# Attention values with the values stationary and the probabilities moving, in three attentions of a two-block transformer kernel

## The chip, the cores and the metric

The kernel runs on one core of a Trainium2 chip. The metric is the device time of one launch in microseconds. The whole of two transformer blocks (512 tokens, width 1024) is one program.

## The reference

The first block has an attention with three branches (compressed, selected and window), a short convolution, an attention over a memory and a gated feed-forward. The second has a banded attention, an mLSTM and a feed-forward of 16384 experts. The change touches three attentions, the window and the selected branch of the first block and the band of the second. Each has 8 heads of 64 and 512 queries; in the first block 4 heads share one group of keys and values. For one branch the reference computes

```python
lg = jnp.einsum('bqghd,bkgd->bqghk', q_c, kw_c).astype(jnp.float32) * scale + bias_w
p_win = masked_softmax(lg, mask_w[:, None, None, :], -1)
o_win = jnp.einsum('bqghk,bkgd->bqghd', p_win, vw_c.astype(jnp.float32))
out = g_c[..., 0:1] * o_cmp + g_c[..., 1:2] * o_sel + g_c[..., 2:3] * o_win
```

What is changed is how the second product, probabilities by values, is placed on TensorE. All of it is in float32.

## The kernel before

The code writes a stream of instructions for each engine by hand, with semaphores between them. Nothing plans the order: on each engine it is the order in the code.

An attention is 32 *units*, one for a tile of 128 queries and one head, in the order of query tiles; eight units of one tile are a *group*, and a group's values fill one PSUM bank, 4 or 5 in turn. A unit of query tile t has n blocks of 128 keys: n = 1, 2, 3, 4 for the four tiles in the selected and the band attention (`causal_blocks`), 1, 2, 3, 3 in the window (`win_blocks`). Units go in pairs. The two units of a pair take their queries and keys from the two halves of the partitions.

- TensorE (`attend` of the tensor block, 2247 to 2294). In turn `pair` it issues the scores of units 2 pair and 2 pair + 1 (`score`, line 2245: 64 rows of the array each, up to 512 moving columns), then, for each half, the values of a unit two pairs back (line 2270: the turned probabilities are stationary, 128 columns, and 64 columns of values move; n matmuls) and the transposes of a unit one pair back (line 2260). A float32 matmul is two records in the trace, a transpose is one. `keep_busy` (line 2124) fills known gaps.
- VectorE (`attend` of the vector block, from 1545) adds the bias to the scores, takes the row minimum and writes the logits to SBUF (line 1560). When a group's eight values are there (`pv_done`) it calls `leave` (1523 to 1543), which multiplies the bank by the reciprocal sums and gates into `o_tok` or `oa_tok` and signals `head_out`.
- ScalarE (`softmax`, from 986) in each turn: the exponential of unit 2 pair (line 982), the copy of the turned probabilities of unit 2 pair - 2 from PSUM to `probT` (line 999), then the same for 2 pair + 1 and 2 pair - 1. Between turns `after` issues other things in the selected attention: high halves of the convolution and squares of `o_tok` rows.
- `probT` has two places, one for each parity of the unit; banks 2 and 3 hold the transposes.

Behind the window TensorE computes the compressed branch's logits (2399 to 2404), VectorE shifts them (1640 to 1643), ScalarE takes their exponential, VectorE sums them (1647) and adds the compressed values to `o_tok` (1541, 1543), and the selected attention's logits follow on VectorE. Behind the selected attention TensorE sums the memory's squares (line 2449), multiplies the convolution's half of the output projection (line 2145), then turns `o_tok` (2437), which VectorE has normalised (1678). Behind the band attention TensorE has one projection (line 2145) before it turns `oa_tok` (2655). A fourth attention (memory, `U_MEM`) uses the same functions and is not changed.

What the sequence of one turn is, in the code:

```python
for half in range(2):
    if pair >= 2:
        values(2 * (pair - 2) + half)
    if (2 if after_turn else 1) <= pair <= units // 2:
        turn_prob(2 * (pair - 1) + half)
```

## Time and profile before

| | us |
|---|---|
| median of 3 runs | 2499.01 |
| lowest, highest | 2495.87, 2500.77 |
| the profiled execution's own time | 2498.93 |
| its span | 2497.1 |
| TensorE (matmul) busy | 2449.4 |
| VectorE, ScalarE, GpSimd busy | 1579.0, 961.2, 1298.8 |

The span runs from the first to the last recorded instruction; 1.8 us of the time lie around it. The page and the timelines give starts in microseconds from the start of the span. PE is TensorE's matmuls, PEld its weight loads, DVE VectorE, ACT ScalarE. In a timeline, neighbouring records of one line are one row: the first number is the first record's start, the second the time to the last one's end, and xN their count. A record's end is modelled, with the pipeline's length in it, so the next row can begin before it; the distance of two starts is the time that a group takes. L2145 is the kernel's main product, used by all projections.

### The profile page before, as it was taken

What the parts mean: (1) busy time and instruction counts of PE and PEld (TensorE: products, weight loads), DVE (VectorE), ACT (ScalarE), POOL (GpSimd) and SP (SyncE); (2) the same over time, 40 slices, a digit from 0 to 9 for tenths busy, and PEclk for the clock granted to TensorE, in tenths of its full rate; (3) what the DMA queues carried; (4) which work ended last, traced back from release to release, by engine and by line L of the source; (5) the groups of instructions that cost most, each with busy time, mean ns of one, the idle gap of its engine ahead of it and who ended that gap; (6) DMA issues with size and microseconds to landing.
All of it is one profiled execution on the core that took longest, in us unless ns stands there. A gap on an engine that the chain in (4) does not pass through costs nothing.

```text
span 2497.1 us, 32817 instructions
## 1 busy us (share of the span) xinstructions
PE 2449.4 (98%) x12349; PEld 2071.3 (83%) x12349; DVE 1579.0 (63%) x2572; ACT 961.2 (38%) x1565; POOL 1298.8 (52%) x686
## 2 busy tenths in 40 slices
PE   9999999999999999999999999999999999999998
PEld 6877766778786777788789999999999888888886
DVE  2246354766402735332479887998940699999995
ACT  3256455222223435523333333434333433333333
POOL 3650323444454433144435787766666576766662
PEclk9999999999999999999999999999999999999999
DMA  5320112665433222122223898999998899999992
GB/s 215 118 76 10 58 62 87 197 197 177 152 103 124 77 84 68 35 93 93 101 85 117 295 299 285 357 353 360 356 324 259 299 363 364 360 369 363 365 364 87
DMA packets 212733, 508.91 MB, mean 204 GB/s; under 512 B 18400, under 2 KB 101344, under 8 KB 212192
## 3 DMA queue, kind: packets, MB, share of 16 engines
q1 hardware_dynamic: 123696, 338.22, 38.9%
q0 software_dynamic: 36864, 134.23, 15.1%
q10 hardware_dynamic: 52016, 34.36, 4.4%
q8 instruction: 99, 1.62, 0.3%
q14 instruction: 58, 0.48, 0.1%
HBM read 454.31 MB, written 52.43 MB: 203 GB/s over the span
## 4 chain that ended last, share of the span: by engine, by line
PE 89%; POOL 3%; DVE 3%; ACT 3%; DMA 1%; issue 1%; ACTq 0%; DVEq 0%; SPq 0%
PE bank L2145 72%; PE bank L2709 3%; PE bank_and L2145 3%; POOL weight_split L823 3%; PE bank L2270 3%; PE bank_and L2113 2%; PE bank L2260 1%; ACT weight_split L964 1%; DMA ring<-weights 1%; PE bank_and L2245 1%; PE bank L2245 1%; PE bank L2124 1%; POOL weight_split L839 0%; PE bank_and L2522 0%; PE bank L2581 0%
## 5 line engine op out<-in xcount | busy, mean ns | idle before, releaser
L2145 PE MATMUL bank<-h_split,weight_split 128*128 128x384 f32 (+1 forms) x5568 | 1134.6, 362 | 16.7 <-POOL weight_split L823 7.6
L2145 PEld LDWEIGHTS bank<-h_split,weight_split 128*128 128x128 f32 x5568 | 994.6, 188 | 130.7 <-POOL weight_split L823 14.7
L823 POOL TENSOR_TENSOR weight_split<-ring,weight_split 128x1024 fp32r<-128x1024 f32 x182 | 454.0, 2495 | 727.2 <-ACT weight_split L964 727.0
L2145 PE MATMUL bank<-late_weight_split,weighted_split 128*128 128x512 f32 x2268 | 514.9, 389 | 0.8 <-DVE weighted_split L2047 0.8
L2145 PEld LDWEIGHTS bank<-late_weight_split,weighted_split 128*128 128x128 f32 x2268 | 425.6, 188 | 89.3 <-issue 1.2
L850 POOL DMA_INDIRECT arena<-weights,arena x256 | 313.4, 1224 | 146.3 <-DVE arena L1899 59.5
L839 POOL TENSOR_TENSOR weight_split<-ring,weight_split 128x1024 fp32r<-128x1024 f32 x129 | 310.4, 2407 | 121.6 <-ACT weight_split L1336 120.8
L964 ACT ACTIVATE weight_split<-ring 128x1024 fp32r<-128x1024 f32 x182 | 191.9, 1054 | 291.0 <-PE bank L2145 273.0
L1336 ACT ACTIVATE weight_split<-ring 128x1024 fp32r<-128x1024 f32 x130 | 137.6, 1059 | 388.2 <-PE bank L2145 377.9
L2041 DVE TENSOR_TENSOR arena<-arena 128x384 f32<-128x384 f32 x128 | 226.9, 1773 | 20.2 <-DMA arena<-expert_acts 19.9
L839 POOL TENSOR_TENSOR late_weight_split<-ring,late_weight_split 128x1024 fp32r<-128x1024 f32 x63 | 151.9, 2411 | 103.5 <-ACT late_weight_split L1336 102.7
L1899 DVE CUSTOM_DVE_ANT_0 arena<-arena,bank_and 128x1024 f32<-128x1024 f32 x128 | 153.0, 1217 | 53.3 <-DMA arena<-weights,arena 52.1
L1370 ACT ACTIVATE weighted_split<-arena 128x384 fp32r<-128x384 f32 x128 | 67.3, 526 | 269.9 <-DVE arena L2041 269.9
L2031 DVE SCALAR_TENSOR_TENSOR bank_and<-arena,bank_and 128x1024 f32<-128x1024 f32 x127 | 162.7, 1281 | 0.9
L1336 ACT ACTIVATE late_weight_split<-ring 128x1024 fp32r<-128x1024 f32 x126 | 132.6, 1052 | 46.5 <-PE bank L2145 45.0
L2145 PE MATMUL bank<-hidden_layer_split,weight_split 128*128 128x512 f32 x528 | 122.3, 392 | 1.3 <-POOL weight_split L823 1.0
L2145 PEld LDWEIGHTS bank<-hidden_layer_split,weight_split 128*128 128x128 f32 x528 | 98.3, 188 | 25.0 <-issue 2.6
L1501 DVE SCALAR_TENSOR_TENSOR arena<-bank,rstd 128x512 f32<-128x512 f32 x42 | 29.0, 691 | 126.0 <-PE bank L2145 117.8
L2047 DVE TENSOR_TENSOR weighted_split<-arena,weighted_split 128x384 fp32r<-128x384 f32 x128 | 74.1, 580 | 47.5 <-ACT weighted_split L1370 47.5
L2709 PE MATMUL bank<-arena 128*128 128x128 f32 x768 | 93.4, 275 | 0.0
L2709 PEld LDWEIGHTS bank<-arena 128*128 128x128 f32 x768 | 92.3, 192 | 0.0
L2270 PEld LDWEIGHTS bank<-arena 128*128 128x128 f32 x528 | 67.4, 191 | 24.9 <-ACT arena L999 16.5
(354 smaller groups left out, 2713.0 us busy)
## 6 DMA issues: line engine op xcount, KB each, us to landing
ring<-weights SPq DMA_DIRECT2D x493, 512.0 KB, 4.5
expert_acts<-arena SPq DMA_DIRECT2D x128, 192.0 KB, 4.2
gates_spread<-arena ACTq DMA_DIRECT2D x24, 1024.0 KB, 12.9
arena<-gates_spread SPq DMA_DIRECT2D x96, 256.0 KB, 6.7
arena<-expert_acts SPq DMA_DIRECT2D x128, 192.0 KB, 6.7
arena<-weights,arena POOLq DMA_INDIRECT x256, 7.2
arena<-bias_sel ACTq DMA_DIRECT2D x1, 2048.0 KB, 7.6
arena<-bias_band ACTq DMA_DIRECT2D x1, 2048.0 KB, 7.9
```

The lines of the kernel that those rows point to most:

```text
L823: nc.gpsimd.tensor_tensor(w_split[:, (count - 1) % 2, 1, :], ring[:, n % RING, :], w_split[:, (count - 1) % 2, 0, :], ALU.subtract).then_i ...
L839: nc.gpsimd.tensor_tensor(w[:, 1, :], ring[:, (BEFORE + e) % RING, :], w[:, 0, :], ALU.subtract).then_inc(w_lo_ready, 1)
L850: nc.gpsimd.indirect_dma_start(gathered_rows[:, j % GR, :], None, expert_rows, bass.IndirectOffsetOnAxis(ap=pick, axis=0)).then_inc(gather ...
L964: a.activation(w_split[:, s % 2, 0, :], ring[:, n % RING, :], ACT.Copy).then_inc(w_high, 1)
L1336: a.activation(split_of(e)[:, 0, :], ring[:, n % RING, :], ACT.Copy).then_inc(w_hi_ready, 1)
L1899: v.tensor_tensor_reduce(rows_, rows_, wide[:, :], 1.0, 0.0, ALU.mult, ALU.add, dots[:, j:j + 1]).then_inc(gather_used, 1)
L2031: v.scalar_tensor_tensor(out=wide[:, :], in0=rows_, scalar=coef[:, j:j + 1], in1=wide[:, :], op0=ALU.mult, op1=ALU.add).then_inc(gather_us ...
L2041: v.tensor_tensor(weighed[:, e % 2, :], act_in[:, e % AS, :], gblk[:, b % 2, :, j], ALU.mult).then_inc(weighed_ready, 1)
L2047: v.tensor_tensor(p_split[:, e % PS, 1, :], weighed[:, e % 2, :], p_split[:, e % PS, 0, :], ALU.subtract).then_inc(p_lo_ready, 1)
L2145: ins = mm(*args, start=start, stop=stop)
L2270: last = mm(bank[4 + g % 2][:, h * HD:(h + 1) * HD], probT[:, u % 2, c * P:(c + 1) * P], vals(i, c), start=(c == 0), stop=(c == blocks(i) ...
L2709: mm(bank[2 + n % 3][:, (t % 4) * P:(t % 4 + 1) * P], hot1[:, t % HOT, :], hot2[:, t % HOT, :], start=True, stop=True).then_inc(hot_used, 1)
```

## The change

The values become the stationary side: for a block of 128 keys and one head, 64 columns of values are loaded and the turned probabilities, 128 columns of queries, move. The result stands with the head's dimension on the partitions, and the two units of a pair write the two halves of the partitions of one bank, at 128 columns for each pair (`values_of_pair`). It is issued for a pair as a whole, behind the scores and ahead of both transposes, and waits for both copies. When a group of eight is complete, ScalarE copies the bank to SBUF (`values_copy`, 512 columns), TensorE turns it back into the same bank with four transposes (`turn_values`), and VectorE's `leave` follows one turn later than before, on `values_turned`. The last group of each attention is copied behind the loop and turned at a place of its own: window's between the compressed logits of tiles 1 and 2, with VectorE's `leave` for it behind the shifted compressed logits; selected's behind the sum of the memory's squares; band's right behind the loop. Window and selected attention get the same arguments as the band in the diff; `places` puts the heads in their order in the bank.

```diff
+        values_nsa, values_band = in_h(0, T), at(7616, T)
...
+        values_out = sem("values_copied")
+        values_turned = sem("values_turned_back")
...
+            def values_copy(u0, g0, done, dst, n):
+
+                act_e.wait_ge(pv_done, u0 + NH * (n + 1))
+                wait(act_e, values_turned, done + n)
+                a.activation(dst, bank[4 + (g0 + n) % 2][:, :], ACT.Copy).then_inc(values_out, 1)
+
-            def softmax(u0, units, blocks, col, after=None, begun=0):
+            def softmax(u0, units, blocks, col, after=None, begun=0, copy=None):
 
                 for pair in range(units // 2 + 1):
+                    if copy and pair > 4 and (pair - 2) % 4 == 0:
+                        copy((pair - 2) // 4 - 1)
...
                     if after:
                         after(pair)
+                if copy:
+                    copy(3)
...
-            softmax(U_BAND, 32, causal_blocks, lambda i: i, begun=2)
+            softmax(U_BAND, 32, causal_blocks, lambda i: i, begun=2,
+                    copy=lambda n: values_copy(U_BAND, G_BAND, 8, values_band, n))
...
-            def attend(u0, units, per, blocks, bias, col, done, after=None):
+            def attend(u0, units, per, blocks, bias, col, done, after=None, turned_=None, later=0):
 
-                for pair in range(units // 2 + 3):
+                late = 1 if turned_ is not None else 0
+                for pair in range(units // 2 + 3 + late):
...
-                    behind = 2 * (pair - 2)
-                    if behind > 0 and behind % per == 0:
+                    behind = 2 * (pair - 2 - late)
+                    if behind > 0 and behind % per == 0 and behind <= units - later * per:
                         n = behind // per - 1
-                        dve.wait_ge(pv_done, u0 + (n + 1) * per)
+                        if late:
+                            dve.wait_ge(values_turned, turned_ + n + 1)
+                        else:
+                            dve.wait_ge(pv_done, u0 + (n + 1) * per)
                         done(n)
...
-            attend(U_WIN, 32, NH, win_blocks, win_bias, lambda i: i // NH * NH + nsa_unit(i)[1], window_out)
+            attend(U_WIN, 32, NH, win_blocks, win_bias, lambda i: i // NH * NH + nsa_unit(i)[1], window_out,
+                   turned_=0, later=1)
+            dve.wait_ge(prob_turned, U_SEL)
             for t in range(NT):
                 dve.wait_ge(cmp_logits, t + 1)
...
                 v.tensor_tensor(x, x, low_.unsqueeze(2).to_broadcast([P, NH, 32]),
                                 ALU.subtract).then_inc(cmp_shifted, 1)
+            dve.wait_ge(values_turned, 4)
+            window_out(NT - 1)
...
             def attend(u0, g0, units, per, q, k, blocks, head, vals, before_turn=None, begun=0, busy=(0, 0),
-                       after_turn=None):
+                       after_turn=None, upright=None):
...
+                def values_of_pair(pair):
+
+                    u, g = u0 + 2 * pair, g0 + 2 * pair // per
+                    q0 = 2 * pair % per // 2 * P
+                    pe.wait_ge(probT_ready, u + 2)
+                    if 2 * pair % per == 0 and g >= 2:
+                        pe.wait_ge(head_out, g - 1)
+                    n = blocks(2 * pair)
+                    for c in range(n):
+                        for half in range(2):
+                            last = mm(bank[4 + g % 2][half * HD:(half + 1) * HD, q0:q0 + P], vals(2 * pair + half, c),
+                                      probT[:, (u + half) % 2, c * P:(c + 1) * P], start=(c == 0), stop=(c == n - 1))
+                            if c == n - 1:
+                                last.then_inc(pv_done, 1)
...
+                    if upright and pair > 4 and (pair - 3) % 4 == 0:
+                        upright((pair - 3) // 4 - 1)
+                    if upright and pair >= 2:
+                        values_of_pair(pair - 2)
                     for half in range(2):
-                        if pair >= 2:
+                        if pair >= 2 and not upright:
                             values(2 * (pair - 2) + half)
...
+            def turn_values(g0, done, values, places):
+
+                def turn_group(n):
+                    pe.wait_ge(values_out, done + n + 1)
+                    for m in range(4):
+                        last = nc.tensor.transpose(places(bank[4 + (g0 + n) % 2], m), values[:, m * P:(m + 1) * P], ident)
+                    last.then_inc(values_turned, 1)
+
+                return turn_group
...
                     last = mm(by_group[:, h], qk[:, h, t * P:(t + 1) * P], kcmp_diag, start=True, stop=True)
                 last.then_inc(cmp_logits, 1)
+                if t == 1:
+                    turn_window(3)
...
             mm(bank[7][:, 0:NM], ones, mem_acc, start=True, stop=True).then_inc(sq_summed, 1)
+            turn_selected(3)
...
-                   after_turn=lambda: pe.wait_ge(*taken(first["qk2"] + 7)))
+                   after_turn=lambda: pe.wait_ge(*taken(first["qk2"] + 7)), upright=turn_band)
+            turn_band(3)
```

## Rows read from the trace of the kernel before

**Rows 1.** The page, busy time of each engine and chain that ended last
```profile
PE 2449.4 (98%) x12349; PEld 2071.3 (83%) x12349; DVE 1579.0 (63%) x2572; ACT 961.2 (38%) x1565; POOL 1298.8 (52%) x686
...
PE 89%; POOL 3%; DVE 3%; ACT 3%; DMA 1%; issue 1%; ACTq 0%; DVEq 0%; SPq 0%
```

**Rows 2.** Table of stretches: engine busy us (instructions), granted clock, DMA share, GB/s
```profile
160.00:201.00 41.00, 39.77 (x287) 29.35 (x286) 19.62 (x72) 29.48 (x98) 14.64 (x17) 1.00 0.16 53
...
366.00:400.00 34.00, 30.72 (x95) 18.40 (x95) 11.62 (x18) 21.67 (x35) 9.03 (x6) 0.90 0.10 31
996.00:1036.00 40.00, 40.00 (x299) 30.37 (x298) 16.26 (x64) 28.86 (x92) 1.91 (x1) 1.00 0.09 28
```

**Rows 3.** Timeline of TensorE in the band attention: start us, us, line, records
```profile
997.57 0.49 PE L2245 MATMUL bank_and<-arena 64*128 64x128 f32 x4
...
1023.56 1.13 PE L2245 MATMUL bank<-arena 64*128 64x512 f32 x4
1024.62 1.10 PE L2270 MATMUL bank<-arena 128*128 128x64 f32 x8
1025.57 0.61 PE L2260 MATMUL bank<-const,arena 128*128 128x128 f32 x4
1026.01 1.00 PE L2270 MATMUL bank<-arena 128*128 128x64 f32 x8
1026.85 0.61 PE L2260 MATMUL bank<-const,arena 128*128 128x128 f32 x4
1027.39 1.13 PE L2245 MATMUL bank_and<-arena 64*128 64x512 f32 x4
```

**Rows 4.** Timeline of TensorE at the ends of the three attentions
```profile
164.25 0.43 PE L2270 MATMUL bank<-arena 128*128 128x64 f32 x2
...
200.90 1.95 PE L2403 MATMUL bank<-arena 128*128 128x64 f32 x16
...
204.47 3.65 PE L2124 MATMUL bank<-const 128*128 128x512 f32 x8
...
219.78 0.43 PE L2270 MATMUL bank<-arena 128*128 128x64 f32 x2 [0.28 <-ACT arena L999]
...
258.58 0.65 PE L2449 MATMUL bank_and<-hT,const 128*128 128x256 f32 x2
...
996.80 0.43 PE L2270 MATMUL bank<-arena 128*128 128x64 f32 x2
...
1035.45 4.81 PE L2145 MATMUL bank<-h_split,weight_split 128*128 128x512 f32 x20
```

**Rows 5.** ScalarE's groups of instructions by form, 994.9 to 1036
```profile
L982 ACT ACTIVATE arena<-arena 128x512 f32<-128x512 f32 x8 | 5.7, 716 | 4.2 <-DVE arena L1560 4.2
...
L999 ACT ACTIVATE arena<-bank 128x512 f32<-128x512 f32 x8 | 4.7, 592 | 1.4 <-PE bank L2260 1.4
...
L982 ACT ACTIVATE arena<-arena 128x128 f32<-128x128 f32 x6 | 2.4, 395 | 0.6 <-DVE arena L1560 0.6
...
L999 ACT ACTIVATE arena<-bank 128x128 f32<-128x128 f32 x8 | 2.1, 257 | 0.0
```

**Rows 6.** Timeline of ScalarE beside the pairs of four blocks
```profile
1026.21 0.60 ACT L999 ACTIVATE arena<-bank 128x512 f32<-128x512 f32 x1
1026.70 0.71 ACT L982 ACTIVATE arena<-arena 128x512 f32<-128x512 f32 x1
...
1027.49 0.60 ACT L999 ACTIVATE arena<-bank 128x512 f32<-128x512 f32 x1
1029.28 0.72 ACT L982 ACTIVATE arena<-arena 128x512 f32<-128x512 f32 x1 [1.19 <-DVE arena L1560]
```

**Rows 7.** Timeline of VectorE behind the window and behind the selected attention
```profile
202.15 0.41 DVE L1640 TENSOR_TENSOR arena<-bank,arena 128x256 f32<-128x256 f32 x1
...
210.04 0.69 DVE L1541 TENSOR_TENSOR sq<-bank,arena 128x512 f32<-128x512 f32 x1 [0.50 <-PE bank L2410]
...
262.00 1.67 DVE L1678 TENSOR_SCALAR arena<-arena 128x512 f32<-128x512 f32 x4 [1.36 <-ACT arena L1109]
```

More of the change, by code:

```diff
@@ L1073, in beside_window @@
                     weight_high(first["w_out"])
-            softmax(U_WIN, 32, win_blocks, win_col, after=beside_window, begun=2)
+            softmax(U_WIN, 32, win_blocks, win_col, after=beside_window, begun=2,
+                    copy=lambda n: values_copy(U_WIN, G_WIN, 0, values_nsa, n))
             for t in range(NT):
@@ L1101, in _ @@
             softmax(U_SEL, 32, causal_blocks, lambda i: 32 + i // NH * NH + nsa_unit(i)[1],
-                    after=beside_selected)
+                    after=beside_selected, copy=lambda n: values_copy(U_SEL, G_SEL, 4, values_nsa, n))
             root(2, D, NM)
@@ L1674, in _ @@
             attend(U_SEL, 32, NH, causal_blocks, sel_bias, lambda i: 32 + i // NH * NH + nsa_unit(i)[1], selected_out,
-                   after=split_conv)
+                   after=split_conv, turned_=4)
             dve.wait_ge(o_rms, 1)
@@ L1855, in _ @@
             attend(U_BAND, 32, NH, causal_blocks, lambda i: bias_band[:, i % NH, 384 - P * (i // NH):T], lambda i: i,
-                   lambda t: leave(G_BAND + t, NH, NH * t, oa_tok[:, t, :].rearrange("p (h d) -> p h d", h=NH)))
+                   lambda t: leave(G_BAND + t, NH, NH * t, oa_tok[:, t, :].rearrange("p (h d) -> p h d", h=NH)),
+                   turned_=8)
             def ya_value(c, out_):
@@ L2292, in attend, with heads_four_apart, heads_in_order @@
                         keep_busy(busy[pair], (3, 5)[pair])
+            def turn_values(g0, done, values, places):
[5 more added lines that the diff above has]
+                return turn_group
+            def heads_four_apart(b, m):
+                return b.rearrange("p (s m d) -> p m s d", s=2, m=4)[:, m]
+            def heads_in_order(b, m):
+                return b[:, m * P:(m + 1) * P]
+            turn_window = turn_values(G_WIN, 0, values_nsa, heads_four_apart)
+            turn_selected = turn_values(G_SEL, 4, values_nsa, heads_four_apart)
+            turn_band = turn_values(G_BAND, 8, values_band, heads_in_order)
             def turn_chosen(t):
@@ L2397, in _ @@
                    lambda i, c: nsa_v(i, 1, first_near(i) + c),
-                   before_turn=lambda: pe.wait_ge(*taken(first["vtok"] + 3)), begun=2, busy=(0, 2))
+                   before_turn=lambda: pe.wait_ge(*taken(first["vtok"] + 3)), begun=2, busy=(0, 2),
+                   upright=turn_window)
             pe.wait_ge(logits_ready, U_SEL)
@@ L2427, in _ @@
             attend(U_SEL, G_SEL, 32, NH, nsa_q, lambda i: nsa_k(i, 0, 0), causal_blocks, nsa_head,
-                   lambda i, c: nsa_v(i, 0, c), busy=(4, 0))
+                   lambda i, c: nsa_v(i, 0, c), busy=(4, 0), upright=turn_selected)
             def turn_merged():
```

## The prediction

> **What bounds the kernel now.** I read the page first: TensorE is busy for 98% of the span and is 89% of the chain that ended last [rows 1]. So a microsecond taken from or put on TensorE's path counts whole, unless another engine has become the one waited for. Next the table of stretches, to see what the attentions are (window and band stand in the rows, selected is like band): 41 and 40 us with TensorE full, ScalarE busy for three quarters of the time, VectorE for under half, TensorE's clock at its upper level of 2.4 GHz [rows 2]. Then the order of TensorE's work inside them [rows 3], which is a loop over pairs of units: scores of a pair, values of one unit, transposes of one, values, transposes.
>
> Write n for the blocks of 128 keys (1 to 4). One loop turn at n=4 runs from 1023.56 to 1027.39, 3.83 us: scores 1.06, values 0.95, transposes 0.44, values 0.84, transposes 0.54. There is no wait in it: TensorE bounds the loop. The eight value records of one unit come 0.11 us apart, as do the four transposes; each record has 128 stationary columns, and only 64 moving ones.
>
> The scores show what two tiles of the array do. A pair's four records take 1.13 us busy and 1.06 to the next group. One full record of 512 columns alone streams in 0.43 us: eight take 3.65, (3.65 - 0.60)/7 = 0.436 [rows 4]. Four in a row would be 1.72. So the two scores, which use different halves of the rows, run side by side: two streams of 0.43 and 0.2 us around them, half before (a weight load with nothing to hide under) and half behind. At n=1 the same group is 0.49 busy instead of 1.13, so 0.42 to the next. It is 0.21 + 0.21 n.
>
> **The loop that the change closes.** Before, the values of unit 2p wait for one copy of its turned probabilities, and 0.84 + 0.44 us of other work follow before the second unit's. The change puts both units' values in one block behind one wait for both copies, and both transposes in a row behind it. ScalarE's order stays: exponential, copy a, exponential, copy b. So in each turn: values, transposes of a, copy a, the second exponential, copy b, values. That ring can't be hidden under scores if it is longer than TensorE's own work.
>
> Its parts, from ScalarE's rows [rows 5]: an exponential is 0.40 at n=1 and 0.72 at n=4, 0.29 + 0.107 n. A copy is 0.26 and 0.59, 0.15 + 0.11 n, and the next operation starts 0.10 before its end [rows 6]. Transposes to their end are 0.61 at n=4 [rows 3] and 0.11 less per block, 0.17 + 0.11 n. Copy a starts 0.03 to 0.04 behind them (1026.18 to 1026.21), and I take 0.05 from a copy's end to TensorE.
> - Transposes, handover, copy a, copy b and handover: 0.46 + 0.33 n.
> - The exponential between them: 0.29 + 0.107 n.
> - Values: no row has 64 stationary columns. The bounds are 0.21 + 0.21 n, if the two halves of the columns run side by side as the halves of the rows do (the streams are the same, 2n records of 128 columns each), and 0.21 + 0.43 n, if they run one behind the other (0.107 us per record). I take the first, because a pair of scores is the nearest row; the other stays in the range. Less than 0.21 n can't be, for that is the stream.
>
> The ring is then 0.96 + 0.65 n: 1.61, 2.26, 2.91, 3.56 us. TensorE's own work per turn (values, scores, two transposes) is 0.52 + 0.64 n: 1.16 to 3.08. At each n the ring is 0.45 longer. TensorE would wait about 0.45 us for copy b in each turn, and the period at n=4 falls from 3.83 to 3.56, is about equal at n=3, and rises at n=2 and n=1.
>
> **Sum over an attention,** from the first values to the end of the last. Selected and band have four pairs at each n. Values of 16 pairs: 0.21 x 40 + 0.21 x 16 = 11.8. Transposes and copies in the 14 turns with both: 0.33 x 35 + 0.46 x 14 = 18.0. Exponentials: 0.107 x 38 + 0.29 x 14 = 8.1. The last pair has transposes 0.44, then 0.61 + 0.04 + 0.59 + 0.05: 1.7. Together 39.6. The window has n = 1, 2, 3, 3: 10.9 + 17.0 + 7.7 + 1.4 = 37.0. Before, the same stretches are 164.25 to 200.90 (36.65), 219.78 to 258.58 (38.80) and 996.80 to 1035.45 (38.65) [rows 4]. So +0.4, +0.8 and +1.0: **+2.2 us**. TensorE's saving is eaten by the wait.
>
> **What is added.** 12 groups are copied by ScalarE (512 columns, 0.59) and turned back by TensorE (4 transposes, 0.45).
> - Nine lie inside the loops. Their copies come between copy b and the next first exponential, where ScalarE stands idle (1.19 us before 1029.28, [rows 6]); they cost nothing, and up to 0.2 each if that cover is thinner. Their transposes come between scores and values, in the 0.45 us of waiting; with one more filling of the array I leave 0.1 each: **+0.9**.
> - Window's last group: TensorE turns it between compressed scores. VectorE now starts the compressed logits first, when the first scores are there, 1.1 us behind the last values (200.90) instead of 1.25 (202.15), runs its twelve operations of 0.42 each, 5.1 us, and only then takes the group out, 1.05 us, ahead of the sums. It stands idle 0.50 us for compressed values [rows 7], which absorbs part: 202.0 + 5.1 + 1.05, and 2.4 for sums, reciprocals and products give 210.6 instead of 210.04: **+0.6**.
> - Selected's last group: TensorE waits for the copy (0.2 + 0.6), of which 0.3 us of the memory sum are done, and turns 0.45: the next projection starts **1.0** later. VectorE's rows o_tok, 262.00 to 263.67, are late by 1.3, but TensorE needs them at the end of 5.7 us of projections, moved by 1.0 too; 0.6 of slack is left [rows 7].
> - Band's last group: wait 0.8, turn 0.45, nothing between: **+1.3**. The exit behind it stays under 5.7 us of projection, as now.
> - No DMA is added or moved, and neither SyncE nor GpSimd has an instruction of the change. The window's added wait of VectorE for the last transposes ends before the first compressed scores.
> - VectorE's exits come one turn later and wait for the turning; the scores behind them in its order wait too. They were hidden except around the first window groups. I leave **+0.5**, between 0 and 2.
>
> Sum: 2.2 + 0.9 + 0.6 + 1.0 + 1.3 + 0.5 = **+6.5 us**. The profiled execution took 2498.93 us (span 2497.1); the median of the three runs is 2499.01. So 2505.4. Measurement can tell about 0.2%, 5 us, from no change. With values 0.05 shorter in each of 48 blocks (a lead of half the columns) the sum is +4; with thin covers +11.
>
> The Trainium skill ("TensorEngine Tiling (Array Packing)", section "Performance Considerations") recommends just this exchange of stationary and moving for a moving side of 64 or fewer, with two column tiles, and promises up to twice the speed. For the values alone, 1.79 us at n=4 [rows 3] against my 1.05, that agrees roughly; by the rule applied to the whole loop the first rival below would hold. The same page ("Tiling Modes") says that a change of mode drains the array; the 0.1 us behind each pair of scores agrees with that, and here a third change per turn is added.
>
> **The rivals.**
> 1. *TensorE still bounds the loop, and it is faster.* If ScalarE's copies come in time (the second exponential out of the ring by its place, or handovers shorter than I read), the 0.45 us goes away in 14 turns of three attentions: -18.9. The nine turnings then lie open, 0.55 instead of 0.1: +4.1. Time 2490.5. For it: TensorE is 98% busy, ScalarE has a quarter idle [rows 1, 2]. Against it: ScalarE's strict order, in which 1026.21 copy, 1026.70 exponential, 1027.49 copy stand one behind the other [rows 6]. It decides if the ring is shorter by over 0.45.
> 2. *The halves don't overlap, slower still.* The change then does not do what it says, two heads in two halves at once. Values cost 0.21 n more in each pair, 116 blocks in all: +24.8, together +31: 2530. For it: no row shows column halves, and both streams read all 128 partitions, which the score halves don't. Against it: the rows' halves overlap fully. A partial overlap (a load of weights that isn't hidden, or an issue of 32 instructions that is too slow for 1.05 us) gives half: 2518.
> 3. *Nothing measurable:* the ring's gain at n=4 and the tails cancel, 2497 to 2503.
> 4. *The clock:* after waits it stands at half in a part of 366 to 400, mean 0.90, 3.4 us lost [rows 2]. New waits before the projections of 258 and 1035 could do so: 1 to 4 us on top.
>
> **How the numbers follow.** Forecast (ring bound, halves side by side) 0.55, of which over a third ends under +5; rival 1 0.17; rival 2 0.12, partial overlap 0.10; clock beside it 0.06. Predicted 2505. The range 2492 to 2524 takes in the forecast's own 2502 to 2511, the partial overlap, the clock and the upper half of rival 1; it leaves out full serial order and the rest of rival 1. Faster 0.19, same 0.25, slower 0.56.
>
> **What would show it.** In the profile after: at n=3 and 4 the wait ahead of the values is by ScalarE's copy (line 999 now), near 0.45 us; periods 2.9 and 3.55; value records in two halves that start together, a group of 0.21 + 0.21 n. Without that wait, rival 1; groups of 0.21 + 0.43 n, rival 2. Waits of 0.8 us ahead of the last turning at the end of selected and band. Wrong if the three stretches shrink by over 3 us, or grow by over 8.

## The result and the profile after

The changed kernel takes **2511.14 us** (median of 20 runs, 2506.08 to 2516.05) against 2498.91 for the kernel before (20 runs on the same chip): ratio 1.0048, 95% interval 1.004 to 1.0055. It is slower by 12.2 us; forecast were 6.5, and a range of 2492 to 2524. The profiled execution took 2516.05 us (span 2514.2). First the busy times of the page, and its chain, against [rows 1]:

```profile
PE 2447.8 (97%) x12397; PEld 2053.8 (82%) x12397; DVE 1579.0 (63%) x2572; ACT 970.0 (39%) x1577; POOL 1291.1 (51%) x686
...
PE 87%; ACT 4%; DVE 3%; POOL 3%; issue 2%; DMA 1%; ACTq 0%; DVEq 0%
```

TensorE is busy for 1.6 us less than before, though it carries twelve more turnings, and the span is 17 us longer: its path has got waits. ScalarE's share of the chain went from 3% to 4%; the timelines below show it as the copy for which the values wait. Now the stretches, three of them the attentions, against [rows 2] (columns as there):

```profile
160.00:203.30 43.30, 36.57 (x300) 22.36 (x298) 17.73 (x72) 32.06 (x101) 14.64 (x17) 1.00 0.15 50
215.00:240.00 25.00, 23.20 (x123) 12.37 (x122) 14.17 (x51) 13.62 (x52) 0.00 (x0) 0.80 0.00 1
217.10:267.50 50.40, 44.71 (x326) 26.48 (x325) 26.10 (x87) 35.56 (x109) 0.00 (x0) 0.90 0.00 1
1010.80:1052.80 42.00, 36.02 (x310) 22.50 (x310) 15.97 (x62) 31.26 (x94) 1.52 (x1) 1.00 0.08 26
```

In window (first row) and band (last row) TensorE is now busy for 36.6 of 43.3 and 36.0 of 42.0 us, where it was full. ScalarE is at 32.1 and 31.3 us, still not full. So neither engine is the bound: the dependency between them is. The third row is the selected attention, whose stretch also holds a fall of TensorE's clock, seen in the second (0.80 over 25 us).

TensorE's timeline of the band, first the smallest turn, then the largest ones and the end, against [rows 3] (line 2269 the scores, 2308 the values, 2284 the transposes of the probabilities, 2342 the turning of a group's values):

```profile
1010.78 0.49 PE L2269 MATMUL bank<-arena 64*128 64x128 f32 x4
1011.41 0.44 PE L2308 MATMUL bank<-arena 128*64 128x128 f32 x4
1011.78 0.44 PE L2284 MATMUL bank<-const,arena 128*128 128x128 f32 x2
...
1040.50 1.09 PE L2308 MATMUL bank<-arena 128*64 128x128 f32 x16 [0.38 <-ACT arena L1010]
1041.53 1.09 PE L2284 MATMUL bank<-const,arena 128*128 128x128 f32 x8
1042.55 1.13 PE L2269 MATMUL bank_and<-arena 64*128 64x512 f32 x4
1043.61 0.66 PE L2342 MATMUL bank<-const,arena 128*128 128x128 f32 x4
1044.19 1.09 PE L2308 MATMUL bank<-arena 128*64 128x128 f32 x16
1045.22 1.09 PE L2284 MATMUL bank<-const,arena 128*128 128x128 f32 x8
1047.75 1.09 PE L2308 MATMUL bank<-arena 128*64 128x128 f32 x16 [1.44 <-ACT arena L1010]
...
1052.42 0.66 PE L2342 MATMUL bank<-const,arena 128*128 128x128 f32 x4 [0.72 <-ACT arena L993]
1052.84 0.47 PE L2169 MATMUL bank<-h_split,weight_split 128*128 128x512 f32 x1
```

- A values group (both heads of a pair) moves 128 columns per record and has 64 stationary ones: 16 records at n=4, and 1.03 us to the next group (1044.19 to 1045.22); at n=1 four records and 0.37. Before, the values of two units took 1.79 at n=4 (0.95 and 0.84, [rows 3]). Added up for the line, 160 records of 128 columns cost 12.3 us of busy time in the band; one behind the other at the 0.107 us of a record they would be 17.
- Ahead of the values at 1040.50 stands the wait for ScalarE's copy, 0.38 us. The next turn holds a turning (line 2342, 0.59 us to the next group) and no wait, and is 3.69 long; the one after that, without a turning, 3.56.
- The end: 0.72 us of waiting for the last group's copy, then its turning, and the projection from 1052.84.

ScalarE between 1042 and 1044, against [rows 6], shows the ring (line 985 the exponential, 1010 the copy):

```profile
1042.22 0.60 ACT L1010 ACTIVATE arena<-bank 128x512 f32<-128x512 f32 x1 [0.52 <-PE bank L2284]
1042.71 0.71 ACT L985 ACTIVATE arena<-arena 128x512 f32<-128x512 f32 x1
...
1043.42 0.59 ACT L1010 ACTIVATE arena<-bank 128x512 f32<-128x512 f32 x1
```

Copy a starts 0.04 us after the end of its transposes (which begin at 1041.53), the second exponential stands behind it, then copy b, and TensorE's values follow at 1044.19. The order is as before the change; what is new is that both copies and the exponential between them lie between two groups of values.

For the comparison of all runs I read six stages from TensorE's timelines (us; window: from the third pair's scores to the compressed part; compressed: to selected's first scores; selected: first scores to the end of the values; tail: to the convolution's first product; then to the memory's scores; band: third pair's scores to the next projection). "12" is the unchanged kernel profiled again, the last of the runs below.

| kernel | window | compressed | selected | its tail | to memory | band |
|---|---|---|---|---|---|---|
| before | 37.08 | 13.26 | 44.42 | 0.30 | 86.81 | 39.07 |
| after | 39.37 | 13.80 | 50.38 | 1.21 | 88.17 | 42.06 |
| after, again (12) | 39.41 | 13.79 | 47.04 | 1.20 | 88.26 | 42.04 |

In run 12 the stages add up to 10.8 us above the kernel before, in the profile of after to 14.1. Between them lies one stretch whose code is unchanged and whose length differs all the same: from the memory's scores to the third pair of the band it is 650.7 us before, 653.9 in after, 650.4 in run 12, and between 647.3 and 653.9 in all profiles. So a sum of stages and the length of a whole profile can differ by 3 us in either direction.

### The profile page after: what moved, and what is told of

The parts are those of the page before. It is cut to its first block, busy times and chain, and to the rows that moved or that the text cites. A ratio compares the mean times of both kernels' runs of the same rounds, so it can differ in the third digit from the quotient of the medians.

```text
span 2514.2 us, 32937 instructions
## 1 busy us (share of the span) xinstructions
PE 2447.8 (97%) x12397; PEld 2053.8 (82%) x12397; DVE 1579.0 (63%) x2572; ACT 970.0 (39%) x1577; POOL 1291.1 (51%) x686
## 3 DMA queue, kind: packets, MB, share of 16 engines
q8 instruction: 100, 1.64, 0.3%
## 4 chain that ended last, share of the span: by engine, by line
PE 87%; ACT 4%; DVE 3%; POOL 3%; issue 2%; DMA 1%; ACTq 0%; DVEq 0%
PE bank L2169 72%; PE bank L2777 3%; PE bank_and L2169 3%; POOL weight_split L826 3%; PE bank_and L2137 2%; PE bank L2308 1%; ACT weight_split L967 1%; PE bank L2284 1%; ACT arena L985 1%; ACT arena L1010 1%; DMA ring<-weights 1%; PE bank L2148 1%; PE bank_and L2269 1%; PE bank_and L2589 0%; DVE h_split L1454 0%
## 5 line engine op out<-in xcount | busy, mean ns | idle before, releaser
L853 POOL DMA_INDIRECT arena<-weights,arena x256 | 304.4, 1189 | 146.7 <-DVE arena L1923 59.9
L2777 PEld LDWEIGHTS bank<-arena 128*128 128x128 f32 x768 | 92.3, 192 | 0.0
L973 ACT ACTIVATE arena<-bank 128x512 f32<-128x512 f32 (+1 forms) x54 | 31.3, 580 | 125.7 <-PE bank L2169 125.7
```

Of the source, the lines that this page charges most:

```text
L853: nc.gpsimd.indirect_dma_start(gathered_rows[:, j % GR, :], None, expert_rows, bass.IndirectOffsetOnAxis(ap=pick, axis=0)).then_inc(gather ...
L2777: mm(bank[2 + n % 3][:, (t % 4) * P:(t % 4 + 1) * P], hot1[:, t % HOT, :], hot2[:, t % HOT, :], start=True, stop=True).then_inc(hot_used, 1)
```

## The experiments

**1 and 2: is it ScalarE's order, and is it the clock?** Two theories for the 12 us: the ring (forecast), and TensorE's clock, if it falls by the new waits. Run 1 puts both exponentials ahead of both copies, so that the exponential leaves the ring; run 2 puts one product that nobody reads into the wait of each pair of the selected attention, except a group's first pair.

Run 1, in ScalarE's softmax of the three attentions:

```diff
+                    if copy:
+                        for i in (2 * pair, 2 * pair + 1):
+                            if begun <= i < units:
+                                exponential(u0, i, blocks, col)
                     for half in range(2):
                         i = 2 * pair + half
-                        if begun <= i < units:
+                        if not copy and begun <= i < units:
                             exponential(u0, i, blocks, col)
```

Run 2, on TensorE, ahead of the wait for the copies:

```diff
+                    if q0 and u0 == U_SEL and pair < 99:
+                        mm(bank[4 + g % 2][:, q0:q0 + P], ones, const[:, 0:P], start=True, stop=True)
                     pe.wait_ge(probT_ready, u + 2)
```

> The changed kernel, with ScalarE's order in the three attentions changed from exponential, copy, exponential, copy to exponential, exponential, copy, copy. Ring theory (the second exponential between the two copies makes TensorE wait about 0.4 us ahead of the values of each pair): the wait nearly goes, periods fall from 2.91 to about 2.5 at n=3 and from 3.57 to about 3.1 at n=4, the band attention from first values to the next projection shrinks from 41.4 by 4 to 6 us, and the kernel is 12 to 18 us faster than the changed one, so 0 to 6 us under the kernel before. Rival (the waits are bound by VectorE's logits or by TensorE's issue): the periods stay within 0.1 us and the time within 3 us of the changed kernel's.

> The changed kernel, with one filler matmul of 128 columns (about 0.4 us) ahead of the wait of each pair's values in the selected attention, except at a group's first pair. Clock theory (the new waits at n=1 let TensorE's clock fall to its lower level from 225.0 for 10.2 us, which makes selected 6 us longer instead of 1): the clock stays at its upper level in most of that stretch, selected loses 3 to 5 us, the kernel's time falls by 2 to 5 us. Rival (the ring alone makes selected long, the clock's fall is harmless, since ScalarE's chain does not depend on it): no change, or 0 to 2 us slower by the fillers that don't fit into the wait.

Measured: run 1 ratio 1.0020 (1.001 to 1.0031), 2502.86 us beside 2497.57; stages 37.38, 45.58 and 39.76 for window, selected, band. Against run 12 the window gives back 2.0 us, the band 2.3 and selected 1.5. Run 2 1.0039 (1.0024 to 1.0053), 2508.04 us; selected 47.79, which is 0.75 longer than in run 12, window and band as in run 12. The turns of run 1 in the band, on TensorE and on ScalarE:

```profile
1019.74 1.13 PE L2273 MATMUL bank_and<-arena 64*128 64x512 f32 x4
1021.28 0.88 PE L2312 MATMUL bank<-arena 128*64 128x128 f32 x12 [0.41 <-ACT arena L1014]
...
1023.11 1.13 PE L2273 MATMUL bank<-arena 64*128 64x512 f32 x4
1024.17 1.09 PE L2312 MATMUL bank<-arena 128*64 128x128 f32 x16
...
1026.22 1.13 PE L2273 MATMUL bank_and<-arena 64*128 64x512 f32 x4
```

```profile
1021.63 0.72 ACT L985 ACTIVATE arena<-arena 128x512 f32<-128x512 f32 x1 [0.40 <-DVE arena L1580]
...
1022.35 0.70 ACT L985 ACTIVATE arena<-arena 128x512 f32<-128x512 f32 x1
...
1023.06 1.05 ACT L1014 ACTIVATE arena<-bank 128x512 f32<-128x512 f32 x2
```

With four blocks TensorE has no wait left ahead of the values at 1024.17, and from scores to scores it is 3.11 us (1023.11 to 1026.22) instead of 3.56. With three blocks one of 0.41 us is left, since now the first copy waits behind the second exponential: 1.54 us from the scores to the values (1019.74 to 1021.28), of which the scores take 1.06. So the ring is most of what costs, and order alone gives over half of the 12 us back. I had expected 4 to 6 us in the band alone, and that was too much: it counted every turn without a wait. Run 2 was expected to gain 2 to 5 us by the clock. It has no fall of the clock in the selected attention, but run 12 hasn't either; it cannot say whether the filler did that.

**3 and 4: one attention alone.** Run 3 has window and selected as before the change, run 4 window and band. For each of them all that the change adds is taken out, on the window (two of the places):

```diff
-            softmax(U_WIN, 32, win_blocks, win_col, after=beside_window, begun=2,
-                    copy=lambda n: values_copy(U_WIN, G_WIN, 0, values_nsa, n))
+            softmax(U_WIN, 32, win_blocks, win_col, after=beside_window, begun=2)
...
-                if t == 1:
-                    turn_window(3)
```

> The change in the band attention alone; window and selected as in the kernel before. By the trace after, band with its tail costs 3.0 us (39.07 to 42.06 from the scores of the third pair to the next projection); my prediction for it was 2.3. So the kernel before plus 2.3 to 3.5 us. Rival (the 12 us are spread over the kernel by something that all three share, for instance the later place of weights or of buffers): more than 5 us.

> The change in the selected attention alone. Ring and tail by my terms cost 2.2 us. If the clock falls at its start here too, 5 to 8 us over the kernel before, with a stretch at the lower level between the start of selected and its pairs of two blocks; if that fall needed the window's change ahead of it, 2 to 3 us and no such stretch.

Measured: band alone 1.0008 (0.9999 to 1.0018), 2499.95 us; selected alone 1.0019 (1.0009 to 1.003), 2503.82. The band's stage is 42.06, as in the full change, and all others are as before: its +3.0 us belong to it alone. Selected alone reads 48.89, with a fall of the clock in it (6.8 us at the lower level), and the tail 1.20. The band's part simply adds to the rest; for selected the fall hides how exactly it does, and the window was not run alone.

**5 and 6: take the values out of the ring.** TensorE does scores, transposes of unit a (the pair's first), values, transposes of unit b. Copy a, and the second exponential, then run beside the values. Run 6 adds the order of run 1.

```diff
-                    if upright and pair >= 2:
-                        values_of_pair(pair - 2)
                     for half in range(2):
+                        if upright and half and pair >= 2:
+                            values_of_pair(pair - 2)
```

> The changed kernel, with TensorE's order in each turn changed from scores, values, transposes a, transposes b to scores, transposes a, values, transposes b. ScalarE's order stays. Ring theory: copy b's chain then runs beside 0.44 + 0.85 + 0.34 us at n=3 instead of 0.85 alone, so the wait ahead of the values goes at n=3 and 4 and keeps 0.3 us at n=1 and 0.15 at n=2; the period falls from 2.91 to 2.5 to 2.6 at n=3 and from 3.56 to 3.1 to 3.25 at n=4, the band attention by 4 us, the kernel by 10 to 16 us against the changed one, to within 3 us of the kernel before. Rival (what the changed kernel waits for is the copies' own rate or VectorE): less than 3 us gained.

> Both orders changed: TensorE's as in the run with the values between the transposes, and ScalarE's two exponentials ahead of the two copies. If the two cures are for the same wait, no better than the better of them by over 2 us; if each leaves waits of its own, 2 to 5 us under the better one. The copies now stand behind both exponentials, which need both logits, so copy a can come late: it may also be 1 to 3 us slower than TensorE's order alone.

Measured: run 5 1.0014 (1.0004 to 1.0024), 2503.28 us beside 2498.96; run 6 1.0015 (1.0007 to 1.0024). That is 8 to 9 us less than the changed kernel; 10 to 16 were expected, and 4 in the band. Stages of run 5: window 37.18, selected 44.69, band 39.53, so 2.2, 2.35 and 2.5 us less than in run 12. TensorE in the band:

```profile
1002.31 0.49 PE L2269 MATMUL bank_and<-arena 64*128 64x128 f32 x4
...
1027.57 1.13 PE L2269 MATMUL bank<-arena 64*128 64x512 f32 x4
1028.63 0.66 PE L2284 MATMUL bank<-const,arena 128*128 128x128 f32 x4
1029.21 1.09 PE L2308 MATMUL bank<-arena 128*64 128x128 f32 x16
1030.24 0.66 PE L2284 MATMUL bank<-const,arena 128*128 128x128 f32 x4
1030.83 1.13 PE L2269 MATMUL bank_and<-arena 64*128 64x512 f32 x4
1031.88 0.66 PE L2342 MATMUL bank<-const,arena 128*128 128x128 f32 x4
...
1040.53 1.86 PE L2169 MATMUL bank<-h_split,weight_split 128*128 128x512 f32 x7
```

No wait is left in the loop at four blocks, and from scores to scores it is 3.26 us (1027.57 to 1030.83), where the loop of before takes 3.83 [rows 3]. From the fourth pair's scores to the last pair's the loop takes 28.52 us (1002.31 to 1030.83), two turnings included, against 29.82 before (997.57 to 1027.39, [rows 3]); from there to the projection 9.70 (to 1040.53) against 8.06 [rows 4]. A turning, as the one at 1031.88, adds 0.44 us to its turn (3.70 from values to values instead of 3.26). The values group still takes 1.03. Moving the values is worth as much as taking the exponential out (run 1), and both together (run 6: stages 37.38, 44.85 and 39.70) no more than the better of them: once the ring is shorter than TensorE's work, shortening it again is worth nothing.

**7, 8: the tails, and the filler again.** Run 7 turns selected's last group among the products of the convolution and band's last group among those of the next projection. Run 8 is run 2 in the second to fourth pair alone.

Run 7, in the projection behind the band, and in the products of the convolution:

```diff
             for m in range(KD):
-                dense(1, h_split)
+                dense(1, h_split, ready=(lambda k: turn_band(3) if k == 2 else None) if m == 0 else None)
...
                         pe.wait_ge(low_ready, split_base[1] + k - 3)
+                        if k == 5:
+                            turn_selected(3)
...
-            turn_selected(3)
...
-            turn_band(3)
```

Run 8:

```diff
-                    if q0 and u0 == U_SEL and pair < 99:
+                    if q0 and u0 == U_SEL and pair < 4:
```

> The changed kernel, with the last group of selected and of band turned back inside the projection that follows (ahead of its second and third chunk) instead of ahead of it, so that the copy's 0.8 us has cover. By the trace after, the turning costs 0.9 and 1.2 us there; 0.45 of each are the transposes and stay. So 0.4 to 0.5 us gained in selected's tail, less up to 0.2 for VectorE's later rows, 0.75 in band's: 1.0 to 1.3 us in all. Rival: the exits to VectorE come later and are waited for, nothing gained.

> The changed kernel, with the filler matmul only in the waits of the second to fourth pair of the selected attention (n=1). Clock theory: no lower clock between 215 and 240 us, selected (from its first scores to the end of its values) 46.5 to 47.3 us instead of 50.4, and the kernel 2.5 to 4 us faster than the changed one. Rival: the stretch at the lower level stays, or goes with no effect on selected's length.

Measured: run 7 1.0043 (1.0029 to 1.0056), 2508.46 us; run 8 1.0048 (1.0034 to 1.0063), 2511.52. The end of the band in run 7:

```profile
1042.86 1.66 PE L2169 MATMUL bank<-h_split,weight_split 128*128 128x512 f32 x6
1044.36 0.60 PE L2342 MATMUL bank<-const,arena 128*128 128x128 f32 x4
1044.72 4.38 PE L2169 MATMUL bank<-h_split,weight_split 128*128 128x512 f32 x18
```

The turning stands between products with no idle time before it; the band's stage is 40.83, down by 1.2, and selected's tail 0.35, down by 0.85. Run 8 was expected to be 2.5 to 4 us faster than the change, and is not. Its selected attention has no fall of the clock, but its window has one (at 180.6 us, 3.4 us long; stage 41.16 instead of 39.4). The filler does not tell what the falls depend on.

**9 and 10: the versions that could win.** Run 9 is 5 and 7 together. Run 10 changes the band alone, with both cures.

> The changed kernel with TensorE's transposes a ahead of the values and both last turnings inside the projections. If the two cures add: window 37.2, compressed part 13.8, selected 44.7 and 0.35, memory part 87.3, band 38.3 us. Against the kernel before that is +0.1, +0.5, +0.3, 0.0, +0.5, -0.8: 0.5 to 2 us slower, not to be told from it. If they don't add, 3 us or more slower.

> The change in the band attention alone, with both cures. From the stages: band 38.3 instead of 39.07 us, so 0.8 us faster than the kernel before, within noise of it. If the change's form cannot gain at all, 39.1 or more.

Measured: run 9 1.0019 (1.0009 to 1.0028), 2501.99 us beside 2497.66; stages 37.24, 13.79, 44.69, 0.35, 88.85 and 38.32. Its attentions are as expected, its time is not: 0.5 to 2 us above before were expected, and it is 4.3. Run 10 1.0005 (0.9993 to 1.0016), 2498.57 us. The band's stage of 38.33 in run 10 is 0.74 below before, as expected, and 0.74 us is not to be seen in the total. Nothing beats the kernel before by what can be measured. The profiled execution of run 10 is also the one that shows a fall of the clock in the window, whose code is that of the kernel before:

```profile
175.00:188.00 13.00, 11.68 (x62) 7.81 (x61) 5.91 (x21) 7.71 (x24) 10.89 (x12) 0.74 0.15 47
```

The stage is 40.78 there, against 37.08. Just ahead of the fall (at 177.8) TensorE waits 1.32 us for its values, where the kernel before waits 0.59; so 0.7 of the 3.7 us are a longer wait. The fall in run 8's window follows a longer wait than usual too, 1.85 us instead of 1.2. But waits of 1.60 and 1.42 us at this place, in runs 1 and 6, had no fall behind them.

**11: the window's extra wait.** In the window one turn was 3.27 us where the ring gives 2.37. VectorE's timeline there, and TensorE's beside it:

```profile
174.44 0.21 DVE L1649 TENSOR_SCALAR arena<-arena 128x96 f32<-128x96 f32 x1
174.68 0.75 DVE L1650 RECIPROCAL arena<-arena 128x96 f32<-128x96 f32 x1
175.47 0.48 DVE L1651 TENSOR_SCALAR arena<-arena,const 128x8 f32<-128x8 f32 x1
175.98 0.20 DVE L1544 RECIPROCAL arena<-arena 128x8 f32<-128x8 f32 x1
176.22 0.42 DVE L1550 TENSOR_TENSOR arena<-arena 128x8 f32<-128x8 f32 x1
176.67 0.69 DVE L1553 TENSOR_TENSOR arena<-bank,arena 128x512 f32<-128x512 f32 x1
177.28 0.55 DVE L1576 CUSTOM_DVE_ANT_0 arena<-bank,arena 128x384 f32<-128x384 f32 x1
```

```profile
177.66 0.92 PE L2269 MATMUL bank_and<-arena 64*128 64x384 f32 x4
179.76 0.66 PE L2308 MATMUL bank<-arena 128*64 128x128 f32 x8 [1.19 <-ACT arena L1010]
```

Three gate operations (lines 1649 to 1651) and the first group's exit stand ahead of the logits of line 1576. They stood between logits before the change as well, and cost TensorE a wait there too, but a shorter one, ahead of its values:

```profile
175.72 0.66 PE L2270 MATMUL bank<-arena 128*128 128x64 f32 x4 [0.59 <-ACT arena L999]
```

Run 11 does the gates while VectorE is idle, after the fourth pair.

```diff
-            def window_out(t):
-                if t == 0:
+            def gates(pair):
+                if pair == 3:
...
+            def window_out(t):
...
 window_out,
-                   turned_=0, later=1)
+                   after=gates, turned_=0, later=1)
```

> The changed kernel, with the three gate operations of VectorE (1.5 us in the trace) done at the fourth turn of the window instead of ahead of the first group's exit. If the late exit of the first group makes the turn of 3.27 us (2.37 by the ring alone), that turn falls to 2.4 to 2.8 and the window from 39.4 to 38.7 or less. Rival: the wait comes from elsewhere (GpSimd's port, ScalarE's cast) and the window stays at 39.3 to 39.5.

> The changed kernel once more. If the clock's fall in selected is a matter of chance from one execution to the next, this profile may have it (selected 50.4 us) or not (47.0 us), with all other stages the same: window 39.4, compressed part 13.8, band 42.1 us. Times between 2505 and 2516 us; their spread is wider than that of the kernel before if so.

Measured: run 11 1.0042 (1.0028 to 1.0056), 2508.55 us; run 12, the change as it is, 1.0048 (1.0035 to 1.0062), 2509.42. The same values group in run 11:

```profile
178.70 0.66 PE L2311 MATMUL bank<-arena 128*64 128x128 f32 x8 [0.28 <-ACT arena L1010]
```

The wait of 1.19 is 0.28, and the window's stage 38.45, down by 0.95: the gates were it, in that turn. By the 0.59 of before, more than half of this 0.95 is a loss that the kernel before has as well. In run 5 the turn at this place is still 3.41 us, and run 9 waits 0.83 in it; runs 9 and 11 together were not tried, though that is the version of the change in all three attentions with the least in its way.

**The clock, from run 12 and all repeats.** The same instructions of the selected attention at two clocks, first after, then run 12:

```profile
223.26 0.44 PE L2308 MATMUL bank<-arena 128*64 128x128 f32 x4 [0.83 <-ACT arena L1010]
...
224.87 0.59 PE L2308 MATMUL bank<-arena 128*64 128x128 f32 x4 [0.38 <-ACT arena L1010]
...
226.01 1.23 PE L2269 MATMUL bank<-arena 64*128 64x256 f32 x4
```

```profile
223.21 0.44 PE L2308 MATMUL bank<-arena 128*64 128x128 f32 x4 [0.83 <-ACT arena L1010]
...
225.56 0.70 PE L2269 MATMUL bank<-arena 64*128 64x256 f32 x4
```

```profile
215.00:240.00 25.00, 21.54 (x141) 11.62 (x139) 15.52 (x55) 16.56 (x63) 0.00 (x0) 1.00 0.00 1
217.00:264.10 47.10, 40.49 (x326) 24.43 (x325) 26.13 (x87) 35.12 (x109) 0.00 (x0) 1.00 0.01 1
```

The two are alike up to 224.87; then the score group of two blocks takes 1.23 us in one and 0.70 in the other. The granted clock of that stretch is 0.80 in one and 1.00 in the other: part of it at 1.2 instead of 2.4 GHz. The wait of 0.83 us ahead of the first values is in both, so the wait alone doesn't decide. Every execution, also the unprofiled ones, has a mean granted clock. Its mean over the runs is 0.9952 for after (20 runs) and 0.9958 for run 12 (5), and 0.9961, 0.9962 and 0.9966 for the kernel before (29, 26 and 21 runs, beside the three sets of experiments). One minus that, times the time, is what the clock can have cost at most: 12.1 and 10.5 us against 9.7, 9.5 and 8.5. And time times clock, what would be left without it, is 2498.8 and 2499.4 against 2488.5, 2489.6 and 2489.5. So of the mean's +12 us, **about 10 are work and waits, and some 2 to 3.5, at most, are clock**.

## Why the prediction was right and wrong

The side was right, and the mechanism, but the size was 6.5 instead of 12. Run 12's timeline accounts for it (after, profiled, has 3.3 us more of clock in selected). The prediction's own sign of being wrong, three stretches that grow by over 8 us from first values to end, is missed by little in run 12 (2.3 + 2.1 + 2.8 = 7.2), and met in after (10.5) by that fall of the clock:

| step | forecast | run 12 |
|---|---|---|
| window: ring, 3 inner turnings, late exits | +0.4, +0.3, share of +0.5 | +2.3 |
| compressed part | +0.6 | +0.5 |
| selected: ring, 3 inner turnings | +0.8, +0.3 | +2.6 |
| its tail | +1.0 | +0.9 |
| band: ring, 3 inner turnings, tail | +1.0, +0.3, +1.3 | +3.0 |
| sum | +6.5 with the +0.5 | +9.4 |
| clock (means over the runs) | 0, a rival of 1 to 4 | about +2 to 3.5, at most |

- **The halves overlap: right.** A values group measured 0.37, 0.59, 0.81 and 1.03, about 0.15 + 0.22 n, 0.05 to 0.02 below the forecast from pairs of scores. Rival 2 falls, its partial form too.
- **The ring: right.** Forecast 0.96 + 0.65 n. The band's turns without a turning measured 1.61, 2.26, 2.91 and 3.56 where both sides have n = 1, 2, 3 and 4 blocks: the same to 0.01. That it agrees so closely is luck in part: the values group is 0.02 to 0.05 shorter than assumed, so the rest of the ring is as much longer. The wait is 0.38 instead of 0.45. Runs 1 and 5 take the ring apart in two ways, and give back 1.5 to 2.3 and 2.2 to 2.5 us per attention. Rival 1 (TensorE the bound, 2490.5) falls as the change stands. It would also have been too good by its own terms. In run 5 TensorE has hardly a wait in the loop but for the gates' turn in the window, and the attentions only come back to the time of before (37.18, 44.69, 39.53 against 37.08, 44.42, 39.07). The rows of run 5 say where the rival's gain went, 16.7 us against before (18.9 less the ring's 2.2), or 5.6 per attention: TensorE's turn at four blocks is 3.26 and not 0.52 + 0.64 x 4 = 3.08, since two groups of transposes each have their own filling (0.59 us for four, against 0.44 right behind values in the kernel before); the turnings cost 0.44 to 0.5 each; and behind the last scores, where nothing covers copies, it is 1.64 longer (9.70 against 8.06), the third turning included, with waits of 0.24, 0.47 and 0.69 for the last copies and 0.72 for the last group's.
- **The failed step: covers taken as nearly free.** For the copies it said "they cost nothing, and up to 0.2 each if that cover is thinner"; it left 0.1 for the transposes of each of nine inner turnings, and +0.5 for VectorE's late exits. A turning took 0.59 us of TensorE, not 0.45, more than the wait of 0.38 that should hide it; such turns were 0.13 to 0.15 longer than the ring, 1.2 in all for the 0.9 of the sum. More was missing elsewhere (run 12). Two turns in which VectorE's exit stands ahead of logits were longer than the ring by 0.94 in window (3.31 for 2.37, with the gates) and by 0.44 in selected (2.81 for 2.37, with a part of the convolution's split), so 1.4 for the +0.5. The window's second turn was longer by 0.43 (2.04 for 1.61): there ScalarE's cast of a weight, 1.05 us (line 967), stands ahead of the next exponential, and the sum had no term for it. Nor had it one for the first values, at which it began: selected's wait 0.83 us for copy b, 0.55 more than before, and the band's come 0.2 later. Forecast and measured stages differ by 9.4 less 6.5, 2.9.
- **Tails: right.** 0.5 for 0.6, 0.9 for 1.0 and 1.2 for 1.3. Run 7 gives back 0.85 and 1.2, though a bit of the first is taken by the next stage (87.36 against 86.8).
- **The clock** was named as a rival and missing from the sum, and its place was wrong: forecast at the projections behind the attentions, a fall was seen in the selected attention in three profiles (after, runs 4 and 11), in the window in runs 8 and 10, and in neither in runs 7 and 12. Both profiles of the changed kernel also have one in the stage to memory (granted clock 0.89 from 324 to 340; stage 88.2 instead of 86.8), and runs 9 and 10 have as long a stage, with a fall there too, without most of the added waits. That the waits cause the extra 2 to 3.5 us is not shown. For it: run 5, without most of them, has a mean clock of 0.9964, as before, and after 0.9952. Against it: run 2, with waits filled in selected alone, has 0.9963 too, and run 10, whose only changed attention has hardly a wait, has 0.9955 over 11 runs, with a fall in code that the change doesn't touch.

**Open.** What sets a fall of the clock. And some 2 us in runs 1, 5 and 9: their stages add up to 3.6, 2.2 and 2.3 us above before, and their medians stand 5.3, 4.3 and 4.3 above those of before. The stages are of one execution each; outside them the code is the same, but not the waits. Behind the memory attention TensorE waits for weights that GpSimd splits (`weight_split`) at a product, at 430.34 us for 1.94 us in run 5, at 429.55 for 1.12 in run 1 and at 430.12 for 1.38 in run 9, where the kernel before has no wait. Nine of the ten profiles with window and selected both changed have this wait of 1.1 to 1.9 us (run 2 has not), and none of before and runs 3, 4 and 10. It would be of the right size; no run tests it.

## What to carry over

Work out a change of loop order as sums, one for each engine and one for each ring of dependencies through several engines, and take the longest at each size. Pairing two units behind one wait shortened TensorE's work here and lengthened the ring, and the ring took more than the work had saved. A pair's operation costs least between the two halves of its successor's work (run 5), not ahead of them; even so it did not beat the kernel before. Where a loop has become bound by a ring, what stands in the ring's path on any engine costs time that slack hid before: a late exit, a cast of weights, a turning longer than the wait that should hold it. Give each a price from a row before calling it hidden.

## What the runs showed of the hardware

- Two tiles of 64 stationary columns, on all 128 rows, with moving sides of 128 columns, run side by side in full: 16 records of 0.107 us of stream in 1.03 us (after, band), and with less around them (about 0.16 us) than two tiles of 64 rows (0.21, [rows 3]).
- Each step from a group of one shape to a group of another costs 0.15 to 0.2 us: 0.16 at the values, 0.21 at the scores, and 0.15 at the transposes, whose eight records take 1.02 us for 0.87 of stream (1041.53 to 1042.55). In the kernel before, four transposes right behind values of the same shape take 0.44, without it.
- TensorE's clock fell for 3.4 to 10.2 us in attention stretches in some executions and not in others of the same program (after and run 12), once in the window of a kernel whose window is that of before (run 10). A single profile of such a kernel is good to some 3 us; the stages of the attentions, read apart from the falls, are good to 0.1 or 0.2.
